# An eleventh weight place and a ninth kept block, paid for with halved attention maps, in a one-core two-layer trunk

## The reference

```python
def token_mixers(h, w_in, w_out, ...):
    dq, dk, dv, sq, sk, sv, iq, ik, iw = jnp.split(h @ w_in, split_points, axis=-1)
    a_out = rms_norm(diff_attention(dq, dk, dv, lam, ...), subln_g) * (1.0 - lam_init)
    b_out = indexed_sparse_attention(sq, sk, sv, iq, ik, iw, ..., topk)
    return jnp.concatenate([a_out, b_out], axis=-1) @ w_out

def peer_ffn(h, w_q, sub_keys, u_tab, v_tab):        # per block of 128 tokens
    s = einsum('thcd,hckd->thck', xt @ w_q, sub_keys)
    s1, i1 = lax.top_k(s[:, :, 0], 16); s2, i2 = lax.top_k(s[:, :, 1], 16)
    best, pos = lax.top_k(s1[..., :, None] + s2[..., None, :], 16)
    g = softmax(best); act = gelu(einsum('thkd,td->thk', u_tab[eidx], xt))
    return einsum('thk,thkd->td', g * act, v_tab[eidx])

for i in range(2):
    h = layer_norm(ALPHA * h + token_mixers(h, ...), ln1)
    r = ALPHA * h + peer_ffn(h, ...)
    h = layer_norm(r + sigmoid(r @ ple_wg[i] + ple_bg[i]) * (p[i] @ ple_wp[i]), ln2)
```

## Time and profile before

| | |
|---|---|
| median of 3 runs | 1598.83 us (1597.42 to 1599.74) |
| the profiled execution | 1597.55 us, its span 1595.8 us |
| busy | PE 76%, DVE 66%, ACT 42%, POOL 36% |
| moved | 648.45 MB, 406 GB/s over the span |

### The profile page before, as it was taken

How to read it: one execution, slowest core, us unless ns; L and a number is a source line. 1 busy time by engine, 2 the same in 40 slices (tenths; PEclk the granted TensorE clock), 3 DMA queues, 4 the chain that set the end, 5 groups by cost and what they waited for, 6 DMA issues and landing times.

```text
span 1595.8 us, 22703 instructions
## 1 busy us (share of the span) xinstructions
PE 1213.1 (76%) x8234; PEld 603.9 (38%) x8234; DVE 1045.3 (66%) x2636; ACT 668.6 (42%) x2027; POOL 580.9 (36%) x518
## 2 busy tenths in 40 slices
PE   9999868787868689786895977978798768444556
PEld 9686423333532266231551335524255223000112
DVE  3467997745778664654688684575578958644555
ACT  2323445723344435363344532536344534323444
POOL 0013443443333323343344332334443434544441
PEclk9999989898888899797997978999899876555557
DMA  9869999999999999999999999999999999999996
GB/s 384 360 250 396 396 421 420 421 421 420 421 420 421 417 396 421 421 420 421 421 421 421 421 417 370 420 421 420 422 420 419 420 421 420 422 421 421 421 421 248
DMA packets 91344, 648.45 MB, mean 406 GB/s; under 512 B 10144, under 2 KB 11616, under 8 KB 13152
## 3 DMA queue, kind: packets, MB, share of 16 engines
q0 software_dynamic: 74016, 536.90, 81.3%
q1 hardware_dynamic: 16704, 109.76, 16.8%
q10 hardware_dynamic: 512, 0.34, 0.1%
HBM read 645.91 MB, written 1.05 MB: 405 GB/s over the span
## 4 chain that ended last, share of the span: by engine, by line
DMA 45%; PE 30%; DVE 14%; ACT 7%; issue 3%; POOL 2%; SPq 0%; ACTq 0%; DVEq 0%; POOLq 0%
DMA rows<-uv_dram,rows_of 39%; PE bank L1343 10%; PE acc L1663 7%; DVE rows L1303 7%; PE bank L1361 5%; DMA store<-wmix_dram 4%; POOL rows L622 2%; ACT dg L835 1%; PE acc L1658 1%; ACT L832 1%; ACT ex L748 1%; PE bank L1614 1%; DMA rows<-wmix_dram 1%; ACT gel L832 1%; DMA store<-wclose_dram 1%
## 5 line engine op out<-in xcount | busy, mean ns | idle before, releaser
L622 POOL DMA_INDIRECT rows<-uv_dram,rows_of x510 | 576.7, 1131 | 985.9 <-PE acc L1663 661.3
L1303 DVE CUSTOM_DVE_ANT_0 rows<-rows,hb 128x1024 f32<-128x1024 f32 x384 | 463.9, 1224 | 313.1 <-DMA rows<-uv_dram,rows_of 310.6
L1663 PE MATMUL acc<-rows,dg 64*64 64x512 f32 x3072 | 453.1, 701 | 198.0 <-ACT dg L835 196.2
L832 ACT ACTIVATE gel<-dots 128x1 f32<-128x1 f32 x512 | 102.7, 201 | 630.1 <-DVE dots L1303 628.7
L1663 PEld LDWEIGHTS acc<-rows,dg 64*64 64x64 f32 x3072 | 102.0, 145 | 459.7 <-ACT dg L835 369.3
L1343 PE MATMUL bank<-xT,store 128*128 128x128 f32 x1888 | 235.1, 286 | 15.7 <-DMA store<-wmix_dram 10.4
L1343 PEld LDWEIGHTS bank<-xT,store 128*128 128x128 f32 x1888 | 225.5, 200 | 55.5 <-issue 41.9
L1303 DVE CUSTOM_DVE_ANT_0 rows<-rows,store 128x1024 f32<-128x1024 f32 x128 | 155.5, 1224 | 119.3 <-DMA rows<-uv_dram,rows_of 118.7
L1658 PE MATMUL acc<-rows,dg 128*32 128x256 f32 x1024 | 119.7, 565 | 133.3 <-ACT dg L835 132.8
L835 ACT ACTIVATE dg<-dg,gel 128x64 f32<-128x64 f32 (+1 forms) x512 | 174.7, 341 | 48.4 <-ACT gel L832 1.5
L1361 PE MATMUL bank<-store,xT 128*128 128x512 f32 x352 | 166.3, 618 | 17.2 <-DMA store<-wmix_dram 14.4
(11 more groups left out here) (230 smaller groups left out, 1016.2 us busy)
## 6 DMA issues: line engine op xcount, KB each, us to landing
store<-wmix_dram SPq DMA_DIRECT2D x78, 1024.0 KB, 9.7
store<-wclose_dram SPq DMA_DIRECT2D x15, 1024.0 KB, 10.4
rows<-uv_dram,rows_of POOLq DMA_INDIRECT x510, 16.0
rows<-wmix_dram SPq DMA_DIRECT2D x5, 1024.0 KB, 14.8
rows<-prm_dram SPq DMA_DIRECT2D x2, 1024.0 KB, 19.1
store<-wmix_dram SPq DMA_DIRECT2D x2, 512.0 KB, 9.1
res<-x_dram SPq DMA_DIRECT2D x1, 512.0 KB, 3.7
rows<-wmix_dram SPq DMA_DIRECT2D x1, 512.0 KB, 7.4
```

The costliest lines, as they stand in the source:

```text
L622: pool.indirect_dma_start(out=rows[:, slot, :], out_offset=None, in_=uv_d[phase // TILES], in_offset=bass.IndirectOffsetOnAxis(ap=rows_of[ ...
L832: A(gel[:, s + j:s + j + 1], dots[:, s + j:s + j + 1], ACT.Gelu).then_inc(gelu_done, 1)
L1303: V.tensor_tensor_reduce(out=rows[:, s, 0:D], in0=rows[:, s, 0:D], in1=tokens, scale=1.0, scalar=0.0, op0=ALU.mult, op1=ALU.add, accum_out ...
L1663: ins = MM(acc[HT * j:HT * j + HT, 512 * r:512 * r + 512], dg[at, s, :], rows[at, s, D + 512 * j:D + 512 * j + 512], start=False, stop=Fal ...
```

## The change

Fewer maps are held at once: `ex` and `probsT` shrink to half, `HELD` = 4 maps. Their room goes to an eleventh place, and pq0a becomes the ninth kept block, so 99 blocks are loaded instead of 101.

- *Halves.* With 256 keys, exps1 writes over the maps of exps0, so it waits for wts0 (now one half of the heads, reciprocals of its own); sexp1 waits for the transposes of spt0; spt1 stands behind the new spv0, and spv1 behind spt1. Scores of groups 3 and 4 (ps3, ps4) go where those of groups 0 to 2 lay, so ACT waits for the choice of the group before last. In the close stage the second half of the norm's parameters goes to `sc`.
- *dk0 and dk1* of the first run are lent places 0 and 1 (`LENT`) instead of ring slots 6 and 7. Their second reading moves from the start to pairs 3 and 9 of phase 1, and the loads that follow into those places wait for it.
- *Places.* For all runs but the first, the block takes the third youngest of the free places (`AHEAD` = 3) instead of the oldest. In phase 2 the loads from the last closing weights to the output projection go round three places, and the others are filled with the queries' blocks from pair 36 on.
- *Plan.* The mix of each run ends two to six pairs later (`behind_mix`, `attend_first`, `attend_last`), and the choosing steps that followed it are packed: more of them fall on the first pairs of the next phase. In phase 3 the projections come as two blocks, a free pair, two blocks. ACT serves C1a of the first run ahead of pq2b.
- *Last phase.* `hx` and the table lie in the three places that are free longest.

```diff
-PLACES = 10
+PLACES = 11
+HELD = 4
...
-    ("spt0", 27, 28, None), ("spt1", 28, 29, None), ("spv", 30, None, None), ("merge", None, None, 32),
+    ("spt0", 27, 28, None), ("sexp1", None, 28, None), ("gb0", 28, 29, None), ("spv0", 29, None, None), ("spt1", 30, 31, None),
+    ("gb1", 31, 32, None), ("mT0", 31, 32, None), ("spv1", 32, None, None), ("mix0a", 33, None, None), ("mix1a", 34, None, None),
+    ("merge", None, None, 34), ("mT1", 35, 36, None), ("mix0b", 36, None, None), ("mix1b", 37, None, None),
...
 SINGLY_PROJECT = [
-    ("T", 12, 13, None), ("par", 12, 13, None), ("idx", 13, 14, None), ("dq0", 14, None, None), ("dq1", 15, 16, None),
-    ("dk0", 16, None, None), ("dk1", 17, 18, None), ("iw", 18, 19, None), ("sq0", 18, None, None), ("sq1", 19, 20, None),
+    ("T", 12, 13, None), ("par", 12, 13, None), ("idx", 13, 14, None), ("dq0", 15, None, None), ("dq1", 16, 17, None),
+    ("dk0", 18, None, None), ("dk1", 19, 20, None), ("iw", 20, 21, None), ("sq0", 21, None, None), ("sq1", 22, 23, None),
 ]
 SINGLY_FIRST = [
-    ("T", 9, 10, None), ("par", 9, 10, None), ("sq0", 11, None, None), ("iw", 13, 14, None), ("sq1", 13, 14, None),
+    ("dk0", 3, None, None), ("dk1", 9, 10, None), ("T", 13, 14, None), ("par", 13, 14, None), ("sq0", 15, None, None),
+    ("iw", 17, 18, None), ("sq1", 17, 18, None),
 ]
...
-EARLY = [(U_IQ, U_IQ + 1), (U_IK,)] + [tuple(units_of(part)) for part in ("dq0", "dq1", "dk0", "dk1")]
-EARLY_SLOTS = (3, 2, 4, 5, 6, 7)
-KEPT_BLOCKS = [(U_SK, U_SK + 1)] + [tuple(units_of(part)) for part in ("pq1a", "pq2a", ...)]
-HX_BLOCKS, SPREAD_BLOCK = 2, 2
-HELD_LATE = (0, 1, SPREAD_BLOCK)
+EARLY = [(U_IQ, U_IQ + 1), (U_IK,)] + [tuple(units_of(part)) for part in ("dq0", "dq1")]
+EARLY_SLOTS = (3, 2, 4, 5)
+LENT = [tuple(units_of(part)) for part in ("dk0", "dk1")]
+KEPT_BLOCKS = [(U_SK, U_SK + 1)] + [tuple(units_of(part)) for part in ("pq0a", "pq1a", "pq2a", ...)]
+AHEAD = 3
...
-                at = min((a for a in range(PLACES) if run is not CLOSE[2] or a not in HELD_LATE), key=lambda a: free[a])
+                if run is CLOSE[2] and not late:
+                    late = tuple(sorted(range(PLACES), key=lambda a: free[a])[:3])
+                open_to = sorted((a for a in range(PLACES) if free[a] < i and a not in late), key=lambda a: free[a])
+                at = open_to[0] if run is MIX[0] else open_to[max(0, len(open_to) - AHEAD)]
...
-        ex = sb("ex", [128, 8, SEQ])
-        probsT = sb("probsT", [128, 16, T])
+        ex = sb("ex", [128, HELD, SEQ])
+        probsT = sb("probsT", [128, 2 * HELD, T])
...
                 if part in ("exps0", "exps1"):
                     act.wait_ge(dmax_ready, n + n // 2 + 1 + half * tile)
+                    if half and tile:
+                        act.wait_ge(dw_ready, DIFF_HEADS * n + DIFF_HEADS // 2)
...
                 if part in ("sexp0", "sexp1"):
+                    if half and tile:
+                        act.wait_ge(*full_at(run, "spt1"))
...
+                    if part in ("ps3", "ps4"):
+                        act.wait_ge(*((rows_picked, len(GROUPS) * n + g - 1) if n < LAST else (chosen_ready, g - 1)))
```

121 lines of the change are left out of this document (71 added, 50 removed), and 28 rows, old and new, of tables (ATTEND_PLAN, FIRST_PLAN).

## The result

The changed kernel takes 1602.95 us (median of 6 runs, 1600.91 to 1604.73) beside 1597.54 us for the kernel before on the same chip (1595.52 to 1599.74). The ratio is 1.0031, 95% interval 1.0021 to 1.0041: **about 5 us slower**. Forecast were 1594 us and a range up to 1601. The profiled execution took 1601.17 us, 1.8 under the median; its span is 1599.3, 3.5 more than before.

The account below looks back on a forecast made before the run. Transfers bound the kernel, at 421.5 MB per ms. Terms -5.0 - 4.5 + 2.5 + 2.5 + 0.5 = -4.0 took 1597.55 to 1593.5 us, or 1594.8 against the median; forecast 1594, range 1589 to 1601.

Parts of the forecast that it names:

- Bytes: Phases 1 and 3: keeping pq0a saves one load each, two times 2.49 us where transfers set the pace: -5.0 us.
- Rival 4: Block loads: each has a real fixed cost, removing it frees at most 4.9 us; 1589 us, chance 0.05.
- Phase 3's projections: Near 970 us: spacing dq0 two pairs behind the index projection ends most of a 5.3 us stall: -4.5 us.
- Rival 2: Phase 3's projections: the stall stays because PE, coming late, reaches dq0 at once; 1598.5 us, no change, chance 0.12.
- The start: Phase 1's first pairs: two blocks move into the gathered part, +5.0, half the shortfall recovered, -2.5: +2.5 us, ends 0 and +5.
- The turn to phase 4: Pair 54 of phase 3 to pair 2: DVE's packed steps put it about 9 us behind, mostly covered: +1.5 us.
- The cover: Turn to phase 4: rows outstanding 16.0 us, four blocks at pair 3 and DVE's free time behind cover DVE's 9 us lag.
- Rival 1: Turns to phases 2 and 4: DVE's backlog is paid in full, +3.5 us at most, no change; chance 0.15.
- its sign that the text gave: Where phase 4 begins: a rate below 410 GB/s with DVE above 95% busy would show rival 1.
- the "slower" rival: Phase 2's projections: three places are too few, 5.3 us of dry transfers a round, up to 1615 us; chance 0.10.
- The turn to phase 2 and its projections: Turn: same DVE steps with late closing weights, +1.0 us, ends 0 and +4; projections: PE waits 4 us once, +0.5.

Follow-up runs that it names:

- group 4 later: Changed kernel with pq4a and pq4b of phase 3 a pair later, group 4's keys two pairs later in phase 4: 1604.12 us, ratio 1.0040.
- DVE's steps alone: Kernel before with only DVE's choosing steps of phase 3 (A, B, C, permutations) moved to the change's pairs: 1605.07 us, ratio 1.0049.
- permutation behind: Changed kernel with DVE reading group 1's permuted list (perm1) behind A2a and A2b in the last phase-3 turn: 1597.53 us, ratio 0.9997.
- phase 4's first pairs spread: Changed kernel with perm1 read behind A2a and A2b, and A3b, B3b, C3 and group 3's permutation later in phase 4: 1596.84 us, ratio 0.9994.
- one step to a pair: Changed kernel with phase 3's group 2 and 3 choosing steps one to a pair, pairs 62 to 9, perm1 behind A2a: 1595.78 us, ratio 0.9987.
- reading a pair later: The run "one step to a pair" with DVE reading perm1 at pair 63 instead of 62: 1595.59 us, ratio 0.9989.
- both edits: Changed kernel with perm1 read behind A2a and A2b, pq4a and pq4b a pair later, group 4's keys two: 1600.92 us, ratio 1.0018.
- PE's crowd away: The run "one step to a pair" with pq4a at pair 62, pq4b at 63, ps4 at 65 and ple at 5: 1596.97 us, ratio 0.9993.

## Why the prediction was wrong, point by point

**Bytes, -5.0.** 646.35 MB were moved, as forecast. The price was measured only roughly: eight kept blocks cost 3.4 with an interval that holds 5.0. Rival 4 would have made it up to 9.8 (two of 4.9); with many transfers in flight the runs don't show it. By the fixed 2.0 us that the Trainium skill (DMA: Bandwidth & Descriptors, "Anatomy of one DMA") gives a DMA on the path through POOL, an estimate for the two is 8.8. These loads are issued by SP, and the runs don't show it for them.

**Phase 3's projections, -4.5.** The size was right, -5.2 in slices 24 and 25, with POOL issuing through PE's wait. But I priced the spacing as if it ended with sq1. It pushes the attention, which lost 2.5 in slices 26 to 29 (0.9 to 3.5 in variants alike there), and the chain to the turn, by three of its five pairs. In the kernel before the same spacing gave nothing (1.0002, 1.0006) or cost time (1.0038). Rival 2 named the right result for the wrong reason: the stall did not stay, it moved.

**The start, +2.5.** It cost 0 in these two traces: the five slices sum to 30.4 before and after. "DVE's pace still limits pairs 5 to 14" was too careful by half: 420 GB/s from 110 to 170. The first pair was on PE at 114.77, forecast near 115.

**The turn to phase 4, part of +2.5 (+1.5, ends 0 and +6).** This is **the step that failed**: +8.9. Its sum of DVE's work was good: 76.1 us from pair 54 to pair 2. DVE took 84.15 (1194.31 to 1278.46), of which 8.01 was the wait for the bank and 1.08 one for a row: 75.1 of work. What failed was to treat the steps as one packed block whose only limit is DVE. The integer tapers of `behind_mix` and `attend_last` took one pair each from perm1's distance, two pairs between PE and DVE before, and so put both into one pair, and DVE's reading ahead of A2a and A2b. I had both rows before me and asked only what they add, not what DVE stands in front of, with what behind it.

The cover failed too. I set the 16.0 us that a row is outstanding against a lag summed over thirteen pairs. But issues come from slots, and a slot comes free when PE has done its products. From pair 61's products to pair 62's it is 12.9 us (1238.28 to 1251.15), where it was 5.4 before; POOL stands 11.59 us without a slot, and what is outstanding lands meanwhile. The variants bear this out: 13.0 and 13.9 us between these products go with POOL waits of 11.74 and 11.96 (group 4 later, DVE's steps alone), 9.7 with 7.5 and 3.5 to 4.4 us short in pairs 63 to 1 (permutation behind, phase 4's first pairs spread, one step to a pair, reading a pair later), 8 with 5.8 and nothing short (both edits, PE's crowd away). The distance of the dots does not decide: with the reading a pair later it is 5.4 us and POOL waits 7.52.

So three things make up the shortage of this turn: the wait with A2a and A2b behind it, PE's crowd ahead of pair 62's products (4.1 us with the wait down to 2.47, none without the crowd), and DVE's packing in phase 4 (2.7 us in pairs 4 and 5, gone when spread). The run with DVE's steps alone loses as much in all.

**Rival 1** was the mechanism nearest to what came, and its sign that the text gave (below 410 GB/s with DVE above 95% busy) is in the window 1260 to 1280; in the deeper hole from 1240 to 1260 DVE was waiting, busy 83%. Its price, +3.5 at most, rested on the same upper end of +6 and was too low. It should have been the "slower" rival; I had put that on phase 2's places, where PE waited 1.8 us for a block once and 0.5 once more.

**The turn to phase 2 and its projections, +1.0 and +0.5.** Together with the rest of phase 1 +4.3. Of this the 2.3 in pairs 3 to 6 come of DVE's packing and the late blocks together (gone when either is). PE's wait of 8.16 us at ple I had not priced. The window 540 to 600 is 397 instead of 401, 0.6 us, as forecast; profiles of kernels alike there read 381 to 404, so that agreement is luck.

Right in the traces, then: the end of phase 3's stall and its size. Wrong: the price of the delay by which it was bought. That the gains hold in time was not shown: without the last turn's +1.5 the sum was -5.5, and the run with PE's crowd taken away, whose last turn is whole, is 1.1 us under the kernel before (0.3 over to 2.6 under).

## What to carry to other kernels

When a table shifts work of several engines, list each pair of producer and consumer that cross engines and their distance in time before and after, and look first at those that become zero: a read that stands ahead of other work on an in-order engine costs its wait, and that of all behind it. Judge cover by the longest single gap between two releases of a slot, not by a lag summed over many. And count a stall that is cured by spacing as moved until the stretches behind it are read too: sum the shortage of the whole span, so that none is left out.
